# A decoder trunk on one core: five pieces of memory attention written as one stage

## The chip, the cores and the metric

The kernel runs on one core of a Trainium2 chip. A core has TensorE (PE, matrix products), VectorE (DVE), ScalarE (ACT), GpSimd (POOL) and SyncE (SP, which here only issues DMAs). The metric is the device time of one execution, in microseconds (us). Lower is better.

## The reference

One step of a one-layer trunk for 1024 prompt tokens and 8 sample tokens, model width 1024: a half-step feed-forward network, an input projection `u @ w_in`, three branches on its result (RWKV-7 time mixing, latent attention, memory cross-attention), a gated merge of the branches, and a second half-step network. The change touches the memory branch alone:

```python
def mem_kv(mem, W):                       # mem: 256 rows of 1024
    m = rmsnorm(mem, W['mem_norm'])
    k = (m @ W['mem_w_k']).reshape(B, M, MEM_HEADS, MEM_HEAD_DIM)   # 4 heads of 128; an output too
    v = (m @ W['mem_w_v']).reshape(B, M, MEM_HEADS, MEM_HEAD_DIM)   # an output too
    return k, v

def mem_attend(q, mem_k, mem_v):
    s = jnp.einsum('bqhd,bkhd->bhqk', q, mem_k).astype(jnp.float32) * (MEM_HEAD_DIM ** -0.5)
    prob = jax.nn.softmax(s, axis=-1).astype(mem_v.dtype)
    return jnp.einsum('bhqk,bkhd->bqhd', prob, mem_v).reshape(B, T, MEM_DIM)
```

The prompt's 1024 queries attend to the `k` and `v` computed here. Each of the 8 sample tokens has one query and its own cached keys and values (256 rows of 4 heads of 128, so 512 KB of keys and 512 KB of values each). All inputs and outputs are float32.

## The kernel before

The program is a row of stages (`@stage`). Each has one block with an instruction stream per engine, tied by semaphores, and ends in a barrier of all engines; inside a stage every engine runs its own list in the order written. `Steps` counts an engine's finished pieces of work, and a wait names a piece. The large arrays A, B, C, W live in one area of on-chip memory and are reused stage by stage. `k.ps[0]` to `k.ps[7]` are the eight PSUM banks, each 128 x 512 float32.

Before the change: `decode_attention` (L2143) runs the samples' attention over paged cache rows; SP issues its page loads in `pages` (L2218), and PE waits for them. Then comes the memory branch: keys, values, norm, prompt attention and sample attention, in four stages:

- `memory_keys` (L2485) loads two row tiles and both weights, turns the rows on PE (16 transposes, L2510), and ends its first block. `rms_norm` (L154, a stage of its own) squares, sums on PE, takes the root and scales. The second block makes the key and value rows with 32 float32 products of 512 columns (L2532), copies them on ACT (L2547), turns the keys (L2538) and stores both.
- `mem_attention` (L2004) loops over four heads, two in a loop body. A head's queries (516 KB) are loaded by SP, and eight tiles of 128 queries follow: score product (L2076, float32, 256 columns), maximum on DVE (L2135, L2136), exponential with its sum on ACT (L2104), reciprocal and scaling on DVE (L2138, L2139), two transposes on PE (L2083), copy on ACT (L2109), two output products (L2091), copy on ACT (L2113). POOL first starts the loads of `u_high`, `u_low` and `inv` (8.8 MB) that the next stage needs.
- `decode_memory` (L2564) does the samples: SP loads keys and values, PE spreads a query over the partitions (L2607), DVE multiplies and sums per head (L2642, L2644), a maximum over everything is taken through a PE transpose (L2610, L2612), ACT takes the exponential (L2629), PE sums (L2614), and 64 products of one column with the values as stationary operand give the result (L2620, scaled at L2662).

`tail` (L3077) follows: the merge loads its first weights (SP, L2705) and starts its products on PE.

A float32 product is two MATMUL records in the trace; a product of operands written as fp32r is one. One float32 operand is kept as a high fp32r part and a low remainder elsewhere in the kernel, and three fp32r products (high by high, high by low, low by high) stand for one float32 product.

Of the kernel before, what the change touches and what calls it, by code (L numbers as in the profile page):

```python
# [14 lines left out]
P = 128  # L15
# [1987 lines left out]
@stage  # L2003
def mem_attention(k):  # L2004


    nc = k.nc
    nq = NQ
    S2 = range(2)
    scale = MEM_SCALE  # L2010
    q_buf = [k.C[:, 13 + s, :] for s in S2]
    k_buf = [k.C[:, 15, s * MEM:(s + 1) * MEM] for s in S2]
    v_buf = [k.C[:, 16, s * 256:(s + 1) * 256].rearrange("p (t c) -> p t c", t=MTOK) for s in S2]
    prob = [k.C[:, 17 + s, 0:MEM] for s in S2]
    probT = [k.C[:, 19 + s, 0:MEM] for s in S2]

    landed = [Count(k, f"mem_q_landed{s}") for s in S2]
    order = []
    for i in range(nq + 2):
        order += [("S", i)] * (i < nq) + [("T", i - 1)] * (1 <= i <= nq) + [("O", i - 2)] * (i >= 2)  # L2020
    pe_s = Steps(k, "mem_products", [(s, x) for s in S2 for x in order], primed=True)
    act_s = Steps(k, "mem_functions", [(s, ("exp", i) if m == "S" else (m, i)) for s in S2 for m, i in order], primed=True)
    dve_s = Steps(k, "mem_softmax", [(s, x) for s in S2 for x in ["q"] + [(m, i) for i in range(nq) for m in ("max", "prob")]],
                  primed=True)
    pool_s = Steps(k, "mem_operands", [("kv", s) for s in S2])
    u_landed = Count(k, "mem_u_landed")
    chain = Count(k, "mem_chain")
    links = [0]
    per_chain = 4 * nq

    with nc.Block() as block:
        @block.sync
        def _(sp):
            with sp.Fori(0, MH // 2) as it:
                for s in S2:
                    pe_s.wait(sp, (s, ("S", nq - 1)), it, before=1)
                    sp.sem_inc(k.settled.sem, 1)
                    dve_s.wait(sp, (s, "q"), it, before=1)
                    sp.sem_inc(k.settled.sem, 1)
                    sp.dma_start(q_buf[s].rearrange("p (a t) -> p a t", a=1), k.mem_q[:, bass.ds(it * 2 + s, 1), :])\  # L2040
                        .then_inc(landed[s].sem, 16)

        @block.gpsimd
        def _(pool):
            pool.dma_start(k.XR[:, 0], k.u_high).then_inc(u_landed.sem, 16)
            pool.dma_start(k.XR[:, 1], k.u_low).then_inc(u_landed.sem, 16)
            pool.dma_start(k.inv, k.inv_spill).then_inc(u_landed.sem, 16)
            with pool.Fori(0, MH // 2) as it:
                for s in S2:
                    pe_s.wait(pool, (s, ("O", nq - 1)), it, before=1)  # L2050
                    pool.sem_inc(k.settled.sem, 1)
                    nc.gpsimd.tensor_copy(k_buf[s].rearrange("p (a t) -> p a t", a=1), k.memT[:, bass.ds(it * 2 + s, 1), :])
                    pool_s.done(nc.gpsimd.tensor_copy(v_buf[s], k.memV[:, :, bass.ds((it * 2 + s) * P, P)]), ("kv", s))
            pool.wait_ge(u_landed.sem, 48)

        @block.tensor
        def _(pe):
            def settled():

                pe.sem_inc(k.settled.sem, 1)  # L2060

            pe_s.prime(pe)
            with pe.Fori(0, MH // 2) as it:
                for s in S2:
                    if s == 0:
                        act_s.wait(pe, (1, ("O", nq - 1)), it, before=1)
                    else:
                        act_s.wait(pe, (0, ("O", nq - 1)), it)
                    pool_s.wait(pe, ("kv", s), it)
                    for m, i in order:  # L2070
                        if m == "S":
                            if i == 0:
                                dve_s.wait(pe, (s, "q"), it)
                            if i >= 2:
                                act_s.wait(pe, (s, ("exp", i - 2)), it)
                            ins = nc.tensor.matmul(k.ps[2 * (i % 2)][:, 0:MEM], q_buf[s][:, i * P:(i + 1) * P], k_buf[s],  # L2076
                                                   start=True, stop=True)
                        elif m == "T":
                            dve_s.wait(pe, (s, ("prob", i)), it)
                            if i >= 1:  # L2080
                                act_s.wait(pe, (s, ("T", i - 1)), it)
                            for b in range(MTOK):
                                ins = nc.tensor.transpose(k.ps[4][:, b * P:(b + 1) * P], prob[i % 2][:, b * P:(b + 1) * P],  # L2083
                                                          k.ident[:, :])
                        else:
                            act_s.wait(pe, (s, ("T", i)), it)
                            if i >= 2:
                                act_s.wait(pe, (s, ("O", i - 2)), it)
# [472 lines left out]


@stage
def decode_memory(k):  # L2564


    nc = k.nc
# [1567 lines left out]
```

## Time and profile before

| | us |
|---|---|
| median of 3 runs | 3678.37 (3677.28 to 3681.39) |
| the profiled execution: its time | 3683.9 |
| its span, first to last instruction | 3682.3 |
| PE busy | 3318.0 (90%) |
| DVE busy | 1646.6 (45%) |
| ACT busy | 934.9 (25%) |
| mean granted TensorE clock | 0.936 of full |

The span is the profiled execution's own; the runs without a profile are a few us shorter. Busy times are per engine and overlap. PE at 90% is a mean over stages: in the two feed-forward networks it never rests, and between them there are stretches where it waits. The granted clock is 1.00 at TensorE's full 2.4 GHz and 0.50 at 1.2 GHz; a value between is a mean over a stretch that had both.

### The profile page before, as it was taken

How to read it: one execution, taken by the hardware profiler on the slowest of the kernel's cores; microseconds unless marked ns; L12 is line 12 of the kernel's file. 1: busy time of each engine (PE TensorE's matmuls, PEld its weight loads, DVE VectorE, ACT ScalarE, POOL GpSimd, SP SyncE). 2: the span in 40 equal slices, each digit the busy share in tenths (PEclk: the TensorE clock that was granted, in tenths of full speed). 3: DMA queues.
4: the chain of work that ended last, by engine and by line, in shares of the span. 5: the costliest groups of instructions: out<-in, count | busy, mean ns of one | idle time of the engine just before them, and what ended most of it. 6: DMA issues, size and time to landing. Idle time of an engine off the chain costs nothing. (4 is left out here: it accounts for less than half of the span.)

```text
span 3682.3 us, 64108 instructions
## 1 busy us (share of the span) xinstructions
PE 3318.0 (90%) x25648; PEld 3061.6 (83%) x25648; DVE 1646.6 (45%) x2870; ACT 934.9 (25%) x1718; POOL 298.8 (8%) x402
## 2 busy tenths in 40 slices
PE   7999999989999777757897777999999899999997
PEld 7999999978998777726776545888889899999997
DVE  4445445555455333355543323222232644554555
ACT  5122122132122111214554321111123412212212
POOL 0000000031011222200001200000002300000003
PEclk8999999989999899967998886999999899999998
DMA  5111111024221100001003532211112311111102
GB/s 175 43 49 46 46 46 46 23 74 143 86 70 53 52 3 3 15 19 49 15 2 91 167 153 100 57 43 43 43 57 63 111 46 46 46 46 48 43 23 92
DMA packets 255409, 218.47 MB, mean 59 GB/s; under 512 B 39378, under 2 KB 232699, under 8 KB 254588
## 3 DMA queue, kind: packets, MB, share of 16 engines
q1 hardware_dynamic: 250684, 197.39, 17.2%
q0 software_dynamic: 3504, 18.42, 1.5%
q8 instruction: 143, 2.34, 0.3%
q14 instruction: 38, 0.31, 0.0%
q10 hardware_dynamic: 1040, 0.00, 0.0%
HBM read 179.81 MB, written 35.96 MB: 59 GB/s over the span
## 5 line engine op out<-in xcount | busy, mean ns | idle before, releaser
L1222 PE MATMUL banks<-XR,wR 128*128 128x344 f32 x6336 | 1004.2, 320 | 12.7 <-DVE XR L1455 7.9
L1222 PEld LDWEIGHTS banks<-XR,wR 128*128 128x128 f32 x6336 | 1000.0, 189 | 13.5 <-issue 10.0
L1222 PE MATMUL banks<-hidR,wR 128*128 128x344 f32 x3168 | 515.7, 323 | 6.0 <-DVE A L1354 6.0
L1222 PEld LDWEIGHTS banks<-hidR,wR 128*128 128x128 f32 x3168 | 505.4, 190 | 11.2 <-DVE A L1354 11.2
L850 PE MATMUL banks<-XR,gateR 128*128 128x344 f32 x2304 | 399.7, 331 | 14.4 <-DVE gateR L2852 7.6
L850 PEld LDWEIGHTS banks<-XR,gateR 128*128 128x128 f32 x2304 | 372.8, 191 | 29.5 <-DVE gateR L2830 7.9
L1354 DVE TENSOR_TENSOR A<-A,banks 128x344 f32<-128x344 f32 x528 | 264.4, 511 | 192.5 <-PE banks L1222 191.5
L850 PE MATMUL banks<-XR,pR 128*128 128x344 f32 (+1 forms) x1944 | 317.6, 325 | 8.0 <-DVE XR L1455 4.4
L850 PEld LDWEIGHTS banks<-XR,pR 128*128 128x128 f32 (+1 forms) x1944 | 311.6, 191 | 15.0 <-issue 10.8
L1307 ACT ACTIVATE sq<-sq 128x344 f32<-128x344 f32 x132 | 65.1, 493 | 1005.3 <-DVE sq L1334 1005.3
L1334 DVE TENSOR_TENSOR sq<-banks,shared 128x344 f32<-128x344 f32 x132 | 68.2, 516 | 417.9 <-PE banks L1222 417.9
L979 POOL TENSOR_TENSOR rs<-rs,sq 128x344 f32<-128x344 f32 x63 | 59.3, 942 | 2096.4 <-ACT sq L968 2092.4
L1326 DVE TENSOR_TENSOR wR<-wraw,wR 128x2048 fp32r<-128x2048 f32 (+1 forms) x66 | 147.0, 2228 | 54.9 <-ACT wR L1303 54.9
L402 PE MATMUL banks<-C 64*64 64x64 f32 x3840 | 139.3, 224 | 27.6 <-DVE C L552 11.3
L402 PEld LDWEIGHTS banks<-C 64*64 64x64 f32 x3840 | 127.9, 139 | 38.3 <-issue 38.3
L2838 DVE TENSOR_TENSOR sq<-banks,shared 128x344 f32<-128x344 f32 x72 | 37.2, 517 | 261.3 <-PE banks L2743 261.3
L2781 ACT ACTIVATE sq<-sq 128x344 f32<-128x344 f32 x72 | 35.4, 491 | 369.1 <-DVE sq L2838 369.1
L402 PE MATMUL banks<-W 64*64 64x64 f32 (+1 forms) x1280 | 97.5, 278 | 32.7 <-issue 17.6
L1303 ACT ACTIVATE wR<-wraw 128x2048 fp32r<-128x2048 f32 (+1 forms) x66 | 122.3, 1854 | 0.2
L402 PEld LDWEIGHTS banks<-W 64*64 64x64 f32 x1280 | 91.6, 161 | 33.7 <-issue 33.7
L2743 PE MATMUL banks<-A,w_o 128*128 128x344 f32 x384 | 118.8, 452 | 0.0
L1311 ACT ACTIVATE hidR<-rs 128x344 fp32r<-128x344 f32 x132 | 64.9, 492 | 151.4 <-DVE rs L1341 151.4
(410 smaller groups left out, 3778.6 us busy)
## 6 DMA issues: line engine op xcount, KB each, us to landing
wraw<-in_ffn_down SPq DMA_DIRECT2D x22, 1024.0 KB, 4.9
wraw<-in_ffn_gate SPq DMA_DIRECT2D x43, 512.0 KB, 3.7
wraw<-in_ffn_up SPq DMA_DIRECT2D x43, 512.0 KB, 4.8
praw<-in_w_in SPq DMA_DIRECT2D x26, 512.0 KB, 4.3
C<-in_cache_mla SPq DMA_DIRECT2D x64, 144.0 KB, 2.7
C<-in_cache_mla POOLq DMA_DIRECT2D x64, 144.0 KB, 2.9
B<-h_spill SPq DMA_DIRECT2D x6, 1376.0 KB, 10.1
h_spill<-A SPq DMA_DIRECT2D x6, 1376.0 KB, 6.3
```

The source lines that it names most:

```text
L402: return nc.tensor.matmul(out, lhsT, rhs, start=start, stop=stop)
L850: ins = k.nc.tensor.matmul(out, parts[:, a, cols], k.XR[:, b, f, grp(g)], start=first and n == 0, stop=last and n == 2)
L979: self.pool_s.done(self.k.nc.gpsimd.tensor_tensor(self.acc[g], self.acc[g], self.slot[g, f], ALU.add), (g, f))
L1222: ins = self.k.nc.tensor.matmul(out, wgt[:, a, cols], x(b)[:, grp(g)], start=first and n == 0, stop=last and n == 2)
L1303: self.act_s.done(nc.scalar.activation(self.wr[u][:, 0, 0:n], self.raw[u][:, 0:n], ACT.Copy), m)
L1307: self.act_s.done(nc.scalar.activation(self.sig[g], self.z[g], ACT.Sigmoid), ("sig", t, g))
L1311: self.act_s.done(nc.scalar.activation(k.hidR[:, 0, t, grp(g)], self.h[g], ACT.Copy), ("hi", t, g))
L1326: self.dve_s.done(nc.vector.tensor_tensor(self.wr[u][:, 1, 0:n], self.raw[u][:, 0:n], self.wr[u][:, 0, 0:n].bitcast(F32), ALU.subtract), m)
L1334: self.dve_s.done(nc.vector.tensor_tensor(self.z[g], k.ps[2 * (n % 2)][:, 0:TG], k.inv[:, grp(g)], ALU.mult), ("z", t, g))
L1354: self.dve_s.done(nc.vector.tensor_tensor(k.A[:, j, grp(g)], k.A[:, j, grp(g)], k.ps[4 + n % 4][:, 0:TG], ALU.add), ("dn", g, j))
L2743: ins = k.nc.tensor.matmul(k.ps[2 * at + 1][:, 0:TG], self.w_o[b][:, f], self.branches[b][0][:, f, grp(g)], start=(f == 0), stop=(f == 3))
L2838: steps.done(nc.vector.tensor_tensor(k.t3[:, at, :], k.ps[2 * at][:, 0:TG], k.inv[:, grp(g)], ALU.mult), ("gate",) + m)
```

## The change

`memory_keys`, its `rms_norm`, `mem_attention` and `decode_memory` are gone, and one stage `memory` does their work, without barriers inside and without loops.

- Loads ahead: at the end of `decode_attention`, SP also issues the memory rows and the key weights (3 MB, into B). The value weights, the queries of all heads (2 MB, one transfer), and the samples' cache rows follow in the new stage; the cache rows go through a ring of seven 512 KB slots, where eight had been loaded for values and four reused for keys.
- Norm: ACT takes the squares' row sums straight from the rows (no PE sums); the gain is applied by DVE as it copies the turned rows, and the inverse root by the copies of key rows (DVE) and value rows (ACT).
- Samples beside the products: a query is spread between the key and value products; DVE multiplies and sums meanwhile.
- Scores: queries and keys are split into high and low fp32r parts, with the scale and a minus sign in the query, so a minimum is the bias as it is; three fp32r products replace one float32 product.
- Two query tiles a step, sixteen steps: scores two steps ahead, exponentials one ahead; one reduction, two exponentials, one reciprocal, two scalings, four transposes, one copy of 512 columns, two output products of 256 columns, one copy.
- Waits of a step n: PE's transposes wait for DVE's scaled n, its scores n + 2 for ACT's exponential n, its output products for ACT's copy of the transposes n and for the output copy n - 1. ACT runs exponential n + 1, copy n, output copy n; DVE runs minimum n + 2, scaling n + 1. The samples' pieces lie inside steps: a maximum through PE in steps 0 and 1, the sum in step 2, output products before `output` in steps 4 and 6, their copies on ACT in steps 5 and 7, and the turning back (PE, DVE) in steps 8 and 9.
- Sample output: weights padded to 32 columns are the stationary operand and the values the moving one; four samples use four groups of 32 output partitions, 16 products of 512 columns in all, then eight transposes.
- `u_high` is loaded after the value products, `u_low` after the last sample product (it shares room with three of the ring slots).

The removed functions are printed above. The core of what is added:

```diff
@@ decode_attention, SP
             for n in range(2, N):
                 pages(sp, n, 0)
+            for dst, src in k.mem_loads:
+                sp.dma_start(dst, src).then_inc(k.mem_ahead.sem, 16)
@@ memory, SP
+            def fetch(i):
+                if i >= RING:
+                    if i - RING < DEC:
+                        dve_s.wait(sp, ("s", i - RING))
+                    else:
+                        pe_s.wait(sp, "o%d" % ((i - RING) % DEC // 4))
+                sp.dma_start(slots[i % RING], cache_rows(i)).then_inc(ring_landed[i % RING].sem, 16)
+            sp.dma_start(k.qm_dec[:, :, :], k.mem_q[:, :, SEQ:T]).then_inc(landed_q.sem, 16)
+            for i in range(2):
+                fetch(i)
+            sp.dma_start(w_v, k.io["mem_w_v"][0].rearrange("(f p) n -> p f n", p=P)).then_inc(landed_v.sem, 16)
+            for i in range(2, 4):
+                fetch(i)
+            sp.dma_start(k.mem_raw, k.mem_q[:, :, 0:SEQ]).then_inc(landed_all_q.sem, 16)
+            for i in range(4, 2 * DEC):
+                fetch(i)
@@ memory, POOL
+            pe_s.wait(pool, ("V", 1))
+            pool.dma_start(k.XR[:, 0], k.u_high).then_inc(u_landed.sem, 16)
...
+            pe_s.wait(pool, "o1")
+            pool.dma_start(k.XR[:, 1], k.u_low).then_inc(u_landed.sem, 16)
@@ memory, PE, setup
+            rows("K", w_k, 0, 5)
+            laid(0)
+            laid(1)
+            rows("K", w_k, 1, 6)
+            laid(2)
+            laid(3)
+            keys_turned(0)
+            pe.wait_ge(landed_v.sem, 16)
+            rows("V", w_v, 0, 2)
+            laid(4)
+            laid(5)
+            keys_turned(1)
+            rows("V", w_v, 1, 3)
+            laid(6)
+            laid(7)
@@ memory, PE, a step
+            def score(n):
...
+                for x in X2:
+                    at = (2 * j + x) * P
+                    for m, (a, b) in enumerate(((0, 0), (0, 1), (1, 0))):
+                        ins = nc.tensor.matmul(k.ps[n % 2][:, x * MEM:(x + 1) * MEM], k.mem_qp[a][:, h, at:at + P],
+                                               k.mem_kT[:, b, h, :], start=(m == 0), stop=(m == 2))
...
+            def sample_out(z):
...
+                        ins = nc.tensor.matmul(k.ps[6 + z][32 * s:32 * s + 32, :], scz[:, b, t, :],
+                                               slots[(DEC + b) % RING][:, t, :], start=(t == 0), stop=(t == MTOK - 1))
...
+            score(0)
+            score(1)
+            for n in range(STEPS):
+                turn(n)
+                if n + 2 < STEPS:
+                    score(n + 2)
...
+                output(n)
@@ memory, ACT, a step
+            exponent(0)
+            for n in range(STEPS):
+                if n + 1 < STEPS:
+                    exponent(n + 1)
+                pe_s.wait(act, ("t", n))
...
+                act_s.done(nc.scalar.activation(k.mem_pT[:, n % 2, :], k.ps[2 + n % 2], ACT.Copy), ("t", n))
...
+                pe_s.wait(act, ("o", n))
...
+                act_s.done(nc.scalar.activation(out[:, h, 2 * j * P:(2 * j + 2) * P], k.ps[5][:, 0:2 * P], ACT.Copy), ("o", n))
@@ memory, DVE, setup and steps
+            sampled(0)
+            sampled(1)
+            keys(0)
+            sampled(2)
+            keys(1)
+            sampled(3)
+            keys_low(0)
+            sampled(4)
+            sampled(5)
+            query_low(0)
+            query_low(1)
+            sampled(6)
+            keys_low(1)
+            sampled(7)
+            query_low(2)
+            query_low(3)
...
+            top(0)
+            top(1)
+            scaled(0)
+            for n in range(STEPS):
+                if n + 2 < STEPS:
+                    top(n + 2)
+                if n + 1 < STEPS:
+                    scaled(n + 1)
@@ build
-        memory_keys(k, v["mem_norm"])
-        mem_attention(k)
-        decode_memory(k)
+        memory(k, v["mem_norm"])
         tail(k, v)
```

## Rows read from the trace of the kernel before

**Rows 1.** The page, part 1: engine, busy us, share of the span, instructions.

```profile
PE 3318.0 (90%) x25648; PEld 3061.6 (83%) x25648; DVE 1646.6 (45%) x2870; ACT 934.9 (25%) x1718; POOL 298.8 (8%) x402
```

**Rows 2.** Windows by stage: from:to, length, busy us (instructions) per engine, granted clock, DMA.

```profile
2106.00:2127.00 21.00, 8.04 (x37) 7.12 (x37) 5.25 (x14) 6.63 (x14) 0.00 (x0) 0.58 0.70 250
2127.00:2160.00 33.00, 31.01 (x72) 13.85 (x72) 0.00 (x0) 3.37 (x6) 0.00 (x0) 0.92 0.09 33
2160.00:2168.00 8.00, 0.05 (x1) 0.05 (x1) 0.17 (x1) 1.28 (x1) 3.01 (x7) 0.67 0.75 271
2168.00:2239.00 71.00, 49.94 (x256) 35.06 (x256) 33.37 (x131) 35.03 (x129) 1.49 (x4) 0.89 0.31 126
2239.00:2269.00 30.00, 18.27 (x26) 5.48 (x27) 20.45 (x20) 0.84 (x2) 0.00 (x0) 0.54 0.75 280
2269.00:2297.00 28.00, 27.25 (x129) 27.16 (x128) 0.79 (x3) 0.00 (x0) 0.00 (x0) 0.50 0.00 1
2297.00:2304.00 7.00, 0.14 (x1) 0.14 (x1) 1.23 (x1) 1.10 (x2) 0.00 (x0) 0.50 0.87 231
```

**Rows 3.** Timeline, first instruction of the memory stages: start us, length, engine, line.

```profile
2106.26 0.83 SPq L2501 DMA_DIRECT2D W<-in_mem_prompt  x2
```

**Rows 4.** Timeline, the last of the memory stages and the first after.

```profile
2296.35 0.21 DVE L2662 TENSOR_TENSOR C<-banks,W 128x32 f32<-128x32 f32 x1 [26.66 <-PE banks L2620]
...
2297.33 0.38 SPq L2705 DMA_DIRECT2D C<-in_w_in  x1
```

**Rows 5.** Timeline, prompt attention, two tiles in a row.

```profile
2229.67 0.42 DVE L2135 TENSOR_REDUCE nmax<-banks 128x1 f32<-128x256 f32 x1
...
2231.38 0.42 DVE L2135 TENSOR_REDUCE nmax<-banks 128x1 f32<-128x256 f32 x1
```

**Rows 6.** Groups by line and shape, 2091 to 2304 us: xcount, busy us, mean ns.

```profile
L2532 PE MATMUL banks<-C 128*128 128x512 f32 x64 | 30.2, 635 | 4.3 <-PEq L53 4.3
...
L2091 PE MATMUL banks<-C 128*128 128x128 f32 x128 | 21.7, 295 | 0.8 <-ACT C L2109 0.8
...
L2607 PE MATMUL banks<-W,ident 8*128 8x512 f32 x16 | 16.0, 1114 | 4.5 <-DVE W L2644 3.8 <-ACT W L2627 0.7
...
L2104 ACT ACTIVATE C<-banks,nmax 128x256 f32<-128x256 f32 x32 | 15.1, 473 | 34.7 <-DVE nmax L2136 34.7
...
L2083 PE MATMUL banks<-ident,C 128*128 128x128 f32 x64 | 15.1, 320 | 17.4 <-DVE C L2139 16.6 <-DVE qm_dec L2131 0.8
...
L2135 DVE TENSOR_REDUCE nmax<-banks 128x1 f32<-128x256 f32 x32 | 13.4, 420 | 9.8 <-PE banks L2076 9.8
...
L2109 ACT ACTIVATE C<-banks 128x256 f32<-128x256 f32 x32 | 12.0, 374 | 3.0 <-PE banks L2083 3.0
...
L2139 DVE TENSOR_SCALAR C<-C,rsum 128x256 f32<-128x256 f32 x32 | 11.3, 353 | 1.1
...
L2642 DVE TENSOR_TENSOR C<-spare_w,banks 128x1024 f32<-128x1024 f32 x8 | 9.8, 1222 | 9.4 <-DMA spare_w<-in_cache_mem_k 9.0
...
L2644 DVE TENSOR_REDUCE W<-C 128x8 f32<-128x1024 f32 x8 | 9.8, 1220 | 0.3
...
L2547 ACT ACTIVATE C<-banks 128x512 f32<-128x512 f32 x4 | 2.4, 598 | 34.2 <-PE banks L2532 34.2
```

**Rows 7.** Timeline, PE: 48 fp32r products of 256 columns (prompt latent attention).

```profile
1886.56 5.92 PE L3594 MATMUL banks<-mla_w,XR 128*128 128x256 f32 x48
```

**Rows 8.** Timeline, PE: eight float32 products, 32 output partitions each (page attention).

```profile
2039.32 1.05 PE L2315 MATMUL banks<-C,sq 128*32 128x256 f32 x16
```

**Rows 9.** Window of 4 us in prompt attention, its first head.

```profile
2172.00:2176.00 4.00, 3.76 (x15) 2.83 (x14) 2.19 (x8) 1.59 (x8) 0.00 (x0) 0.50 1.10 462
```

**Rows 10.** Timeline, SP: the last loads of cache pages.

```profile
2061.92 25.65 SPq L2218 DMA_DIRECT2D C<-in_cache_mla  x18
```

**Rows 11.** DMA issues, 2091 to 2304 us: xcount, KB each, median us to landing.

```profile
XR<-u_low POOLq DMA_DIRECT2D x1, 4128.0 KB, 25.0
...
C<-in_mem_w_v SPq DMA_DIRECT2D x1, 2048.0 KB, 15.2
```

More of the change, by code:

```diff
@@ L2143, in decode_attention @@
-@stage
 def decode_attention(k):
@@ L3257, in _ @@
             fin.copy_low(dve, 2)
+STEPS = MH * NQ // 2
 def shape_constants():
@@ L4059, in build @@
         k.mla_wk_raw = at("mla_wk_raw", [P, KT * P], at_k + 4 * SEQ + 2 * P)
+        at_m = 2 * DT * T + 12 * T
+        k.mem_kT = at("mem_kT", [P, 2, MH, MEM], at_m, R32)
+        k.mem_v = at("mem_v", [P, MTOK, 512], at_m + 2048)
+        k.mem_raw = at("mem_raw", [P, MH, SEQ], at_m + 3072)[:, :, :]
+        k.mem_qp = [at("mem_q_high", [P, MH, SEQ], (2 * DT + FT) * T, R32), at("mem_q_low", [P, MH, SEQ], at_m + 3072, R32)]
+        k.mem_prob = at("mem_prob", [P, 2, 2, MEM], at_m + 7168)
+        k.mem_pT = at("mem_pT", [P, 2, 512], at_m + 8192)
+        k.mem_so = at("mem_so", [P, 2, 512], at_m + 9216)
         k.mla_v = at("mla_v", [P, NQ, 2 * P], DT * T)
@@ L4066, in build @@
         k.settled = Count(k, "products_may_start")
+        k.mem_ahead = Count(k, "memory_rows_and_weights_ahead")
+        flat_b = k.B[:, :, :].rearrange("p a t -> p (a t)")
+        k.mem_loads = [(flat_b[:, t * D:(t + 1) * D], k.io["mem_prompt"][0, t * P:(t + 1) * P, :]) for t in range(MTOK)]
+        k.mem_loads += [(flat_b[:, 2 * D:2 * D + 4096].rearrange("p (f c) -> p f c", f=DT),
+                         k.io["mem_w_k"][0].rearrange("(f p) n -> p f n", p=P))]
         k.u_high = nc.dram_tensor("u_high", [P, DT, T], F32).ap()
@@ L4072, in build @@
         k.s_dec = k.q_dec[:, 0:RT, :]
-        k.memT = k.C[:, 12, 0:MH * MEM].rearrange("p (h t) -> p h t", h=MH)
-        k.memV = k.C[:, 21, 0:MTOK * 512].rearrange("p (t c) -> p t c", t=MTOK)
+        k.memV = k.mem_v[:, :, :]
+        k.mem_scz = k.spare_w[:, 7168:7680].rearrange("p (b t h) -> p b t h", b=DEC, t=MTOK)
         k.Bc = k.C[:, 2:22, :].rearrange("p a t -> p (a t)")[:, 0:4 * (NPAGE + 1) * CW]\
```

574 lines of the change are left out of this document (282 added, 292 removed).

## The prediction, made before the changed kernel ran

> **What bounds the kernel now.** I read the page's busy times first, then the windows, then the timeline, then the groups. PE is busy 3318.0 of 3682.3 us [rows 1], so only a stretch in which PE rests, runs at the half clock or does avoidable work can be worth much. The windows by stage show such a stretch [rows 2]. The memory stages begin at 2106.26 [rows 3] and the first load of the next stage is issued at 2297.33 [rows 4]: 191.1 us. In them the reader is to see four kinds of loss:
> - 2106 to 2127: PE is busy 8.04 of 21 us; loads, norm and barriers.
> - 2160 to 2168: PE is busy 0.05 of 8 us; the queries are loading.
> - 2168 to 2239: no engine is full (PE 49.9, DVE 33.4, ACT 35.0 of 71 us). Two tiles start 1.71 us apart [rows 5], and that is a round between two engines: maximum 0.42, exponential 0.47, scaling 0.35 [rows 6], and 0.47 for the small instructions and semaphores between them. DVE does not start the next maximum before the scaling.
> - 2239 to 2297: the clock is 0.54 and then 0.50, first under DVE's sample work (20.45 of 30 us), then under 128 MATMULs of one column, which hold PE for 27.25 us. The last DVE instruction waited 26.66 us for them [rows 4].
> Nothing of another stage overlaps this stretch, so what it loses in length the kernel loses.
>
> **The setup of the new stage.** Times are counted from its first instruction (2106.3 before).
> Products: the 32 float32 products of 512 columns took 30.2 us [rows 6]; the clock of 0.92 over 33 us [rows 2] is 5.3 us at half speed, so 2.6 us are clock and one product is (30.2 - 2.6) / 32 = 0.86 us at full clock. A record's mean of 0.635 against a spacing of 0.43 gives 0.2 us of drain after a group. These products stay. A transpose is 15.1 / 64 = 0.24 us; a spread of a query took 16.0 / 8 = 2.0 us, at the half clock [rows 2, 6], and as a float32 product of 512 columns I take 0.86 at full clock. DVE needs 2 x 1.22 and a gap, 2.6 us, per sample.
> PE's order, end by end: 20 transposes 4.8; key product 0 with the same 2.6 us of half clock 14.3; two spreads 16.0; key product 1 22.9; two spreads 24.6; turning 25.1; value product 0 32.0; two spreads 33.7; turning 34.2; value product 1 41.1; two spreads 42.8. DVE follows: samples 0 to 5 fit under PE (the last pair spread by 33.7, done 39, then two query lows of 1.2 us each by 41.4); sample 6 at 44.6, key low 45.3, sample 7 47.9, two query lows 50.4, the samples' maximum and the first minimum 51.3, exponentials 0 at 52.4, scaling 0 at 53.3. So the first turn of the loop starts at 53.3. The bounds: 41 us, PE's work alone, if DVE kept up; 60 if spreads stay near 2.0 and the half clock lasts longer. I take 53.3, since every term but the clock has its row. ACT's squares, root, copies and query highs (12 pieces of 0.6 to 1.1 us) lie inside the products; without that cover they would cost about 10.
>
> **The loop.** A step is two tiles. Two circles can close it.
> PE to DVE: four transposes 0.5; six fp32r products, 48 of which took 5.92 us [rows 7], so 6 x 0.123 = 0.74, and 0.2 drain; minimum over 512 elements 0.69 (between 0.42 for 256 and 1.22 for 1024); reciprocal and two scalings 0.9; semaphore 0.1. Sum 3.1.
> ACT to PE: two exponentials 0.94, copy of 512 columns 0.60, semaphore 0.2, two output products of 0.43 each (half of 0.86) with drain 1.06, copy 0.37. Sum 3.2.
> PE's own work is 0.5 + 0.74 + 0.86 = 2.1 us and hidden in either. From below the step is 2.6 (the circles opened by work that runs ahead), from above 2 x 1.71 = 3.4, no better than now. I take 3.1. Fifteen steps from the first turn to the last: 46.5. After the last turn: 0.6 + 0.6 + 1.06 + 0.4 = 2.8 with semaphores. The minus sign and the scale in the query save one small DVE instruction a tile; that is in the step.
> Extras in the loop, mostly on one of the circles: maximum through PE 0.5 and 1.0 (steps 0, 1), sum, reciprocals and weights 1.2 (step 2), sample products 2 x 1.9, their copies 2 x 0.6, turning back 2 x 0.7. Sum 9.1. The sample product rests on a row: eight float32 products of 256 columns with 32 output partitions each took 1.05 us [rows 8], where eight of 0.43 in a row would be 3.4; so four groups run together, and eight of 512 columns are 2 x 0.86 + 0.2 = 1.9. Were they not together it would be 6.9 each, 10 us more. They replace the 27.4 us of the old output.
>
> **Clock at the loop's start.** Before the first turn PE rests from about 47 (score 1) to 53.3. After the rest at 2160 PE worked at 0.50 in a 4 us window although it was busy 3.76 of it [rows 9], and the mean to 2239 is 0.89 [rows 2]. I add three steps at the half clock, where PE's terms double and a step is 4.3: 3.4 us. The ends are 0 and all steps (rival 2).
> The Trainium skill (TensorE: Matmul & The Clock Gate, Part 4) says that transposes do not count as activity for the clock. By that rule the loop would be likelier to stay at the low level; it gives rival 2 its place. The old attention loop, with two transposes for every three float32 products, has 0.89 in its row.
>
> **Transfers.** The rows and key weights go behind the last page load, which is issued at 2061.92 + 25.65 = 2087.6 [rows 10]. In the old stage 2 MB landed 15.2 us after issue with 3 MB ahead of them [rows 11]; 3 MB issued at 2087.6 are there by 2102.8, before 2106.3. Nothing of the page loop is queued behind them, since they are issued last; the last page shares the wires with them, 0 to 0.5 us. Without this cover the stage would start some 5 us later. The value weights and the queries are 6.1 MB with what is ahead of them; at the 462 GB/s of [rows 9] that is 13 us, at the 271 GB/s of the load-in 23, and they are wanted at 25.1 and 33. Ring slots are refilled by samples done long before: key 7 waits for sample 0, values for samples 1 to 7, and only the last value waits for the first sample product, two steps before its use. On POOL, `u_high` starts at 41. `u_low` waits for the second sample product, 53.3 + 7 x 3.1 + 7 = 82, and with the 25.0 us of [rows 11] is there at 107, before the end. This is the thinnest cover, 8 us; each us beyond it lengthens the stage.
>
> **Sum.** 53.3 + 46.5 + 2.8 + 9.1 + 3.4 + 0.8 (stage end to the next issue, as 2296.56 to 2297.33 in [rows 4]) = 115.9 us against 191.1: 75 us less. The next stage begins with a load and a half clock as before, so nothing more. The profiled execution took 3683.9, so 3609 by its own time; the median of the runs is 5.5 lower, so 3603.
>
> **Rivals.**
> 2. The loop stays at 1.2 GHz: 15 x 1.2 more, 4 on the extras, less the 3.4 counted: 18.6 less gain, 3622. If the setup does so too (27.5 - 2.6 for the products, 9 for the spreads): 34 more, 3656. For it: after 2269 PE is busy 27.25 of 28 us at 0.50, so a busy PE is not always granted 1.00. Against it: key and value products stood at a mean of 0.92, the old loop at 0.89 with a like mix [rows 2].
> 3. The samples are not hidden: each spread waits for the DVE piece two before it, and if products and DVE take turns, 8 x 2.6 = 20.8 return, and with steps of 3.4 another 4.8: gain 49.6, 3629. For it: strict order on every engine. Against it: the order above leaves each spread ready when its turn comes.
> 4. Slower than before: the code of the loop is now straight and must itself be brought in by DMA, in the first 25 us behind 6 MB of data and from 41 on behind `u_high`. If an engine stands at a block of instructions that lands like `u_low`, 25.0 us after its request [rows 11], three such stops eat the 75 us; five would give 3603 + 125 = 3728. Against it: the page attention is straight code too, and its PE products in [rows 8] ran without a gap.
> The Trainium skill (Runtime: NRT & Kernel Launch, Instruction fetch mechanics) says that sequential fetch runs ahead and is mostly hidden, and that a taken branch is what breaks it; by it this rival is nothing.
> 5. The change doesn't do what it says, and another circle (output copy waits for `output`, which waits for the sample product) makes the steps as long as now: within 7 us of zero it could only come out if the setup grew by 60 too.
>
> **How the numbers follow.** Forecast 0.66; rival 2 in the loop 0.16, whole 0.04; rival 3 0.10; rival 4 0.03; rival 5 0.01. The time is the forecast's, 3603. Its own low end is steps of 2.6 and a shorter setup: 7.5 + 5 + 3 less, 3587; the range takes 3585 to 3632, so that rival 2 in the loop and rival 3 are in it. A measurement of this kernel tells 0.2% (7.4 us) from no change. Faster by more: 0.66 + 0.16 + 0.04 + 0.10 less a little, 0.95; same 0.02; slower 0.03.
>
> **What would show it.** The stretch from the first product's transposes to the merge's first load is 116 us; the first scaled tiles come 53 us into it; minima of two-tile steps are 3.1 us apart; key and value products take 30 us in all; a sample product takes 1.9 us; the clock is 1.00 after the first three steps; no wait of PE for a load, and none of the last barrier for `u_low`. The prediction is wrong if steps take 4 us, if PE waits for `laid` or the ring, or if the stretch after 2300 changes its length.

## The result, and the profile after

| | before | after |
|---|---|---|
| median of 4 runs, us | 3679.88 (3677.28 to 3685.25) | 3592.55 (3588.57 to 3601.47) |
| ratio, 95% interval | | 0.9757 (0.9742 to 0.9773) |
| profiled execution: span | 3682.3 | 3594.7 |
| first load of the memory stages to the merge's first load | 191.1 | 103.6 |

The kernel is 2.4% faster: 87.3 us by the medians, 87.6 by the spans. The forecast was 3603 (75 us less), the range 3585 to 3632. The whole difference lies in the stretch: 191.07 - 103.58 = 87.5 us. What follows it has the same length within 1.1 us (1385.0 from the merge's first load to the end of the span before, 1383.9 after).

PE's line of the page, part 1, answers to [rows 1]; PE lost 55 us of busy time, the largest part of it, 24 us, with the one-column products (27.4 us before, two sample products of 1.86 after), and 8 with the spreads (16.0 before, 7.9 after):

```profile
PE 3263.0 (91%) x25508; PEld 3022.9 (84%) x25508; DVE 1639.7 (46%) x2809; ACT 930.2 (26%) x1681; POOL 298.8 (8%) x399
```

The setup, in the timeline of the kernel after (start us, length, engine, line). L3771 are the transposes of the memory rows, L4020 the minimum, L3838 the transposes of a step, called a turn here:

```profile
2091.07 0.43 SPq L2103 DMA_DIRECT2D B<-in_mem_w_k  x1
...
2107.21 0.63 SPq L3736 DMA_DIRECT2D qm_dec<-mem_q  x1
...
2107.26 3.65 PE L3771 MATMUL banks<-ident,B 128*128 128x128 f32 x16 [1.23 <-PEq L53]
```

```profile
2155.69 1.28 DVE L4020 TENSOR_REDUCE rms_col<-banks 128x2 f32<-128x512 f32 x2
...
2158.34 1.12 PE L3838 MATMUL banks<-ident,mem_prob 128*128 128x128 f32 x4 [4.26 <-DVE mem_prob L4028]
```

```profile
2209.63 0.38 ACT L3951 ACTIVATE C<-banks 128x256 f32<-128x256 f32 x1 [1.22 <-PE banks L3847]
2210.79 0.38 SPq L2390 DMA_DIRECT2D C<-in_w_in  x1
```

The key weights are on their way from 2091, and PE starts 0.05 us after the first load of the stage. The first turn of the loop comes at 2158.34, 51.1 us into the stage (forecast 53.3), and the last one at 2207.17 is followed by the merge's load 3.6 us later, as forecast (2.8 + 0.8). Between them are 48.8 us where 59.0 had been forecast.

The windows by part of the new stage (from:to, length; busy us and instructions of PE, its weight loads, DVE, ACT and POOL; granted clock, DMA share, GB/s), to set beside [rows 2]:

```profile
2107.00:2128.00 21.00, 20.74 (x56) 10.71 (x56) 8.38 (x10) 4.36 (x7) 1.07 (x2) 0.87 0.92 334
2128.00:2152.00 24.00, 21.54 (x57) 9.55 (x57) 17.20 (x16) 7.52 (x9) 2.69 (x5) 0.96 0.72 255
2152.00:2158.00 6.00, 2.07 (x10) 1.78 (x9) 5.44 (x10) 1.59 (x7) 0.00 (x0) 0.50 0.96 372
2158.00:2162.00 4.00, 3.66 (x14) 3.37 (x15) 1.48 (x6) 0.94 (x3) 0.00 (x0) 0.50 0.92 313
2162.00:2166.00 4.00, 3.89 (x19) 3.00 (x18) 2.10 (x8) 1.95 (x7) 0.00 (x0) 0.78 0.82 326
2166.00:2170.00 4.00, 3.46 (x25) 3.11 (x26) 2.09 (x7) 2.56 (x11) 0.00 (x0) 1.00 0.00 0
2170.00:2209.00 39.00, 31.20 (x202) 23.79 (x201) 16.50 (x55) 22.57 (x74) 0.54 (x1) 1.00 0.31 123
2209.00:2217.00 8.00, 0.59 (x3) 0.19 (x1) 1.23 (x1) 1.44 (x2) 0.00 (x0) 0.66 0.67 181
```

PE is busy 42.3 of the first 45 us. Then it is busy 2.07 of the 6 us from 2152 to 2158 while DVE, busy 5.44 of them, ends the samples and the low parts; the granted clock is 0.50 (1.2 GHz) there and until 2162, 0.78 to 2166, and 1.00 (2.4 GHz) from then to 2209, the end of the loop; in the window after it, with PE busy 0.59 of 8 us, it is 0.66.

A step in its steady state, from the same timeline:

```profile
2195.15 0.60 PE L3838 MATMUL banks<-ident,mem_prob 128*128 128x128 f32 x4
2195.35 0.39 ACT L3951 ACTIVATE C<-banks 128x256 f32<-128x256 f32 x1 [1.22 <-PE banks L3847]
...
2195.51 0.48 PE L3826 MATMUL banks<-mem_kT,mem_q_high 128*128 128x256 f32 x2
2195.64 0.47 ACT L3930 ACTIVATE mem_prob<-banks,rms_col 128x256 f32<-128x256 f32 x1
...
2196.50 0.69 DVE L4020 TENSOR_REDUCE rms_col<-banks 128x2 f32<-128x512 f32 x1 [1.59 <-PE banks L3826]
2196.53 0.60 ACT L3941 ACTIVATE mem_pT<-banks 128x512 f32<-128x512 f32 x1
...
2197.19 1.13 PE L3847 MATMUL banks<-mem_pT,mem_v 128*128 128x256 f32 x4 [0.73 <-ACT mem_pT L3941]
2197.30 0.61 DVE L4028 TENSOR_SCALAR mem_prob<-mem_prob,rms_col 128x256 f32<-128x256 f32 x2
...
2198.16 0.60 PE L3838 MATMUL banks<-ident,mem_prob 128*128 128x128 f32 x4
2198.36 0.38 ACT L3951 ACTIVATE C<-banks 128x256 f32<-128x256 f32 x1 [1.22 <-PE banks L3847]
...
2198.64 0.47 ACT L3930 ACTIVATE mem_prob<-banks,rms_col 128x256 f32<-128x256 f32 x1
```

ACT starts an exponential at 2195.64, a copy at 2196.53, PE its output products at 2197.19, ACT their copy at 2198.36 and the next exponential at 2198.64: 3.00 us round. ACT rests 1.22 us of it, waiting for PE (in brackets in the answer's row), PE rests 0.73 waiting for ACT, and DVE rests 1.59 before its minimum. DVE's minimum follows the scores and its scaling ends at 2197.91, 0.25 before the next turn.

Groups of the stage (xcount, busy us, mean ns, idle before), the answers to [rows 6]:

```profile
L3847 PE MATMUL banks<-mem_pT,mem_v 128*128 128x256 f32 x64 | 18.8, 419 | 7.8 <-ACT mem_pT L3941 7.8
...
L3790 PE MATMUL banks<-rs,ident 8*128 8x512 f32 x16 | 7.9, 613 | 0.0
...
L3782 PE MATMUL banks<-B 128*128 128x512 f32 x32 | 14.7, 613 | 0.0
```

A spread took 7.9 / 8 = 0.99 us, the output products waited 7.8 us for ACT's copies, and the key and value products took 14.7 + 14.1 = 28.8 us.

The first sample product in PE's timeline:

```profile
2173.24 0.62 PE L3858 MATMUL banks<-C,spare_w 128*32 128x512 f32 x2
2173.26 0.62 PE L3858 MATMUL banks<-sq,spare_w 128*32 128x512 f32 x2
...
2174.56 0.60 PE L3858 MATMUL banks<-C,spare_w 128*32 128x512 f32 x2
2174.57 0.60 PE L3858 MATMUL banks<-sq,spare_w 128*32 128x512 f32 x2
2175.10 1.13 PE L3847 MATMUL banks<-mem_pT,mem_v 128*128 128x256 f32 x4
```

It runs from 2173.24 to the next product's start at 2175.10, 1.86 us (forecast 1.9): eight products of 512 columns in four groups side by side.

### The profile page after: what moved, and what is told of

Read it like the earlier page. It is cut to its first block and busy times, and to the rows that moved or that the text cites. A ratio compares the mean times of both kernels' runs of the same rounds, so it can differ in the third digit from the quotient of the medians.

```text
span 3594.7 us, 63286 instructions
## 1 busy us (share of the span) xinstructions
PE 3263.0 (91%) x25508; PEld 3022.9 (84%) x25508; DVE 1639.7 (46%) x2809; ACT 930.2 (26%) x1681; POOL 298.8 (8%) x399
## 5 line engine op out<-in xcount | busy, mean ns | idle before, releaser
L850 PE MATMUL banks<-XR,gateR 128*128 128x344 f32 x2304 | 398.2, 330 | 14.7 <-DVE gateR L2537 7.9
L402 PEld LDWEIGHTS banks<-C 64*64 64x64 f32 x3840 | 130.3, 141 | 36.6 <-issue 36.6
```

The lines of the kernel that those rows point to most:

```text
L402: return nc.tensor.matmul(out, lhsT, rhs, start=start, stop=stop)
L850: ins = k.nc.tensor.matmul(out, parts[:, a, cols], k.XR[:, b, f, grp(g)], start=first and n == 0, stop=last and n == 2)
```

## The experiments

All start from the changed kernel. For each, the table gives the stretch (the stage's first load to the merge's first load), the time from the stage's first load to the first turn, from the first turn to the last, and the usual step, all from its profile. The effects of most are a few us, under what a single run's time can tell: the start of the stage alone lay between 2100.09 and 2112.24 from run to run, mostly by the page loads before it (the last of them is issued between 2081.5 and 2094.2). The stretch is free of that. Two profiles of the changed kernel gave 103.58 and 103.37.

| kernel | stretch | to first turn | first to last turn | step |
|---|---|---|---|---|
| the changed kernel | 103.6 | 51.1 | 48.8 | 3.00 |
| e1, no sample pieces | 100.9 | 51.3 | 46.0 | 2.87 to 3.01 |
| e2, loads in the stage | 117.5 | 64.9 | 49.0 | 3.00 |
| e3, samples after | 111.8 | 59.9 | 48.3 | 3.00 |
| e4, old output | 122.0 | 51.2 | 67.2 | 3.00 |
| e5, float32 scores | 100.6 | 47.7 | 49.3 | 3.03 |
| e6, late copy | 101.3 | 51.0 | 46.7 | 2.87 |
| e7, minimum after scaling | 103.7 | 51.2 | 48.9 | 3.00 |
| e8, output a step later | 91.8 | 50.8 | 36.6 | 2.01 |
| e9, setup order | 100.7 | 48.4 | 48.7 | 3.00 |
| e10, e8 and e9 | 91.1 | 49.1 | 37.7 | 2.01 |
| e11, one tile an instruction | 104.2 | 50.3 | 50.2 | 3.12 |

My theory, once the profile was there: the parts of the change are right, and the term of the extras is not. What is laid into a loop that one circle closes costs only what exceeds the rest of its engine. The rival was the way of counting in the prediction, and for the loop, another circle than ACT's.

**e1, are the extras free?**

```diff
-    extra = {0: ["mT"], 1: ["mB"], 2: ["sum"], 4: ["o0"], 6: ["o1"], 8: ["turn0"], 9: ["turn1"]}
+    extra = {}
```

(and the same on ACT and DVE)

> The changed kernel without the samples' pieces inside the loop of sixteen steps (maximum through PE, difference, exponential, sum, weights, the sixteen output products, their copies and the turning back); the samples' part of the output is left out, the setup is as it was. Theory (slack): a step is closed by ACT to PE to ACT (two exponentials, copy of 512 columns, two output products, output copy; 3.0 us), and PE and DVE rest in it, so that pieces laid there cost only what exceeds the rest. Then the time from the first turn to the last falls from 48.8 to about 46.7 us and the stretch from the stage's first load to the merge's first load from 103.6 to about 101.5. Rival (the term of the prediction): each piece adds its own length, 9.1 us together; then the stretch falls to about 94.5.

The stretch fell by 2.7 us to 100.9, the time between the turns by 2.8. So all sample pieces in the loop cost 2.8 us, not 9.1. (The samples' output is missing here, so this is no kernel to use.) In the changed kernel a step with a sample product takes 4.06 instead of 3.00, so 1.86 us of products cost 1.06; the steps with copies on ACT (5 and 7) and with the turning back (8 and 9) take 3.00 like the others. Without the pieces the steps 2 to 6 take only 2.87 to 2.92: PE's turn waits for DVE's scaling there (0.43 us, then less from step to step), until PE waits for ACT's copy instead (0.73 at the end) and the step is 3.00. Two circles of nearly the same length lie side by side.

**e2, the loads ahead.**

```diff
@@ decode_attention, then memory, SP
-            for dst, src in k.mem_loads:
-                sp.dma_start(dst, src).then_inc(k.mem_ahead.sem, 16)
...
+            for dst, src in k.mem_loads:
+                sp.dma_start(dst, src).then_inc(k.mem_ahead.sem, 16)
             sp.dma_start(k.qm_dec[:, :, :], k.mem_q[:, :, SEQ:T]).then_inc(landed_q.sem, 16)
```

> The changed kernel with the loads of the memory rows and key weights (3 MB) issued at the start of the new stage instead of behind the last cache pages. Theory: PE and ACT wait for all three transfers; 2 MB behind 1 MB landed 11.9 us after issue in the changed kernel, so the first transposes come about 9 to 10 us later and nothing of that is won back: stretch 103.6 to about 113, page attention unchanged. The prediction's number was some 5 us: 109. Rival: the other loads are pushed back too and the setup waits for the queries, so that it is more than 12 us.

Timeline of this kernel:

```profile
2111.62 1.29 SPq L3735 DMA_DIRECT2D B<-in_mem_prompt  x2
...
2125.12 2.18 PE L3771 MATMUL banks<-ident,B 128*128 128x128 f32 x9 [14.69 <-DMA B<-in_mem_w_k]
```

PE starts 13.5 us after the first load, and the stretch is 13.9 longer; the rest of the setup has its old length (51.4 us from PE's start to the first turn, 51.1 before). Neither number was right. The key weights are issued 1.3 us after the stage's first load and took 12.1 us to land, and PE waits for all of it; with the stage's other loads issued right behind them they were hardly slower than the 11.9 us of the changed kernel. This part of the change is worth 13.9 us, nearly three times what the prediction said for its cover. It costs the page attention nothing that shows: from the issue of the last page load to the stage's first load it is 17.4 us in this kernel, 18.7 in the kernel before, and 17.2 to 19.2 in those with the 3 MB issued ahead.

**e3, samples beside the products.**

```diff
-            sampled(0)
-            sampled(1)
             keys(0)
-            sampled(2)
             keys(1)
...
+            for b in B8:
+                sampled(b)
```

(the same order in `laid` on PE; the low parts come before the samples)

> The changed kernel with the samples' spreads and their DVE work all after the four products of keys and values, the rest in the old order. Theory: the products come 6 spreads (5.7 us) earlier, then DVE needs 8 x 2.57 = 20.6 us, while keys' and queries' low parts are already done: the first minimum comes about 6 us later than in the changed kernel, and PE, resting longer, starts the loop at the half clock for longer, 1 to 3 us: stretch 103.6 to 111 to 113. Rival (price of the prediction's rival 3): laying the samples beside the products hides their whole 20.8 us: stretch about 124.

8.2 us longer, as the theory had it: 8.7 of it up to the first turn, 0.5 won back behind it. The clock at the loop's start was no worse (48.3 from turn to turn). Laying the samples beside the products is worth 8 us and not 21, because the spreads push the products back (the value products end 39.5 us into the stage in the changed kernel, 33.4 here) and DVE's last pieces are bare in either order (7.0 us from PE's last spread to the first minimum in the changed kernel).

**e4, the old output form.**

```diff
-                        ins = nc.tensor.matmul(k.ps[6 + z][32 * s:32 * s + 32, :], scz[:, b, t, :],
-                                               slots[(DEC + b) % RING][:, t, :], start=(t == 0), stop=(t == MTOK - 1))
+                            ins = nc.tensor.matmul(k.ps[6 + z][:, s * MH + h:s * MH + h + 1],
+                                                   slots[(DEC + b) % RING][:, t, h * P:(h + 1) * P], scz[:, b, t, h:h + 1],
+                                                   start=(t == 0), stop=(t == MTOK - 1))
```

> The changed kernel with the samples' output in the old form: 128 MATMUL records of one column with the values as stationary operand, in steps 4 and 6, in place of the sixteen products in four column groups; no turning back. The old form took 27.4 us at the half clock, 0.43 us a product. Theory: its cost is the weight loading and goes with the clock, so here at full clock 0.21 a product, 13.7 us for all 64, less the 2.1 that the new products cost: stretch 103.6 to about 115. Rival: one-column products let the clock fall to 0.50 and stay 0.43: 27 us, stretch about 129.

PE's timeline, and the windows around it, of this kernel:

```profile
2174.67 3.63 PE L3858 MATMUL banks<-spare_w,C 128*128 128x1 f32 x32
2178.16 6.23 PE L3858 MATMUL banks<-spare_w,sq 128*128 128x1 f32 x32
2184.25 2.05 PE L3847 MATMUL banks<-mem_pT,mem_v 128*128 128x256 f32 x4
```

```profile
2171.00:2176.00 5.00, 4.28 (x35) 3.92 (x33) 2.50 (x9) 3.29 (x12) 0.00 (x0) 1.00 0.02 3
2176.00:2184.00 8.00, 8.00 (x52) 8.00 (x52) 0.29 (x2) 0.00 (x0) 0.00 (x0) 0.69 0.00 0
...
2196.00:2200.00 4.00, 4.00 (x22) 4.00 (x21) 0.00 (x0) 0.00 (x0) 0.00 (x0) 0.51 0.01 4
```

18.4 us longer, between the two. The first 32 records take 3.63 us (0.11 each, half of the old 0.21 a record), the next 32 take 6.23. In the window from 2176 PE is busy 8.00 of 8 us at a granted 0.69, and from 2196 at 0.51. So both theories are true one after the other: a record costs by the clock, with the weight loads busy as long as PE (8.00 of 8 us too), and in this loop, whose clock stays at 1.00 without the form, the clock falls under it while PE never rests.

**e5, float32 scores.**

```diff
-                    for m, (a, b) in enumerate(((0, 0), (0, 1), (1, 0))):
-                        ins = nc.tensor.matmul(k.ps[n % 2][:, x * MEM:(x + 1) * MEM], k.mem_qp[a][:, h, at:at + P],
-                                               k.mem_kT[:, b, h, :], start=(m == 0), stop=(m == 2))
+                    ins = nc.tensor.matmul(k.ps[n % 2][:, x * MEM:(x + 1) * MEM], k.mem_qp[0][:, h, at:at + P].bitcast(F32),
+                                           k.mem_kT[:, 0, h, :].bitcast(F32), start=True, stop=True)
```

(and no `keys_low`, `query_low`)

> The changed kernel with one float32 product for a tile's scores in place of three fp32r products, and without the low parts of queries and keys on DVE. Theory: in the loop PE rests 0.73 us a step before the output products, and four records of 256 columns at a quarter rate are 0.85 us against 0.65 to 0.75 now, so the step stays 3.0; in the setup DVE has two query lows (2.4) and a key low (0.7) less between the last spread and the first minimum: stretch 103.6 to about 100.5. Rival: the circle PE score, DVE minimum, DVE scaling, PE turn is as tight as ACT's, and the longer score makes the step 3.1 to 3.2: the gain of the setup is given back.

100.6 against 100.5 expected. The first turn is 3.5 us earlier and the loop 0.5 longer. The split in three fp32r products loses 3 us here: PE has the time for the float32 ones in the loop, and DVE, which makes the low parts, is the engine that ends the setup.

**e6 and e7, which circle closes the step?**

```diff
@@ e6: ACT
-                pe_s.wait(act, ("o", n))
+                    pe_s.wait(act, ("o", n - 1))
@@ e6: PE
-                if n:
-                    act_s.wait(pe, ("o", n - 1))
+                if n >= 2:
+                    act_s.wait(pe, ("o", n - 2))
...
-                    ins = nc.tensor.matmul(k.ps[5][:, 0:2 * P], k.memV[:, t, n // 4 * P:(n // 4 + 1) * P],
+                    ins = nc.tensor.matmul(k.ps[(5, 7)[n % 2]][:, 0:2 * P], k.memV[:, t, n // 4 * P:(n // 4 + 1) * P],
@@ e7: DVE
-                    top(n + 2)
                 if n + 1 < STEPS:
                     scaled(n + 1)
+                if n + 2 < STEPS:
+                    top(n + 2)
```

> The changed kernel with ACT's output copy one step later, behind the next exponentials and the next copy of transposes, and the output products in two banks in turn. This opens the circle through ACT. Theory: the circle turn n, score n+2, minimum n+2, scaling n+1, turn n+1 stands at 2.9 in the trace (2195.15 to 2198.04) and closes the step then: 2.9 us, stretch about 102. Rival: ACT's circle was the only one, and the step falls to what PE or ACT need, 2.2: stretch about 92.

> The changed kernel with DVE's minimum of a step behind the scaling of the step before, as in the old loop, so that DVE and ACT take turns again; still two tiles a step. Theory: that round is two exponentials 0.99, reciprocal and scalings 0.81, minimum 0.69 and semaphores, about 2.6 us, less than the 3.0 that ACT's circle takes: nothing changes in the loop (48.8 from first to last turn), and running ahead was worth nothing, two tiles an instruction was the gain. Rival: running ahead broke the old round, and without it two tiles take 2 x 1.71 = 3.4 again: 6 us more.

Both came out by the theory. With ACT's circle open the step is 2.87: the circle of turn, score, minimum, scaling was right behind it, and PE's turn now waits for DVE, as it did not before. A turn in PE's timeline of e6:

```profile
2174.83 0.66 PE L3839 MATMUL banks<-ident,mem_prob 128*128 128x128 f32 x4 [0.40 <-DVE mem_prob L4034]
```

With DVE's run-ahead taken back nothing changes (103.7, 48.9). So the run-ahead of the minimum, which looks like the heart of the new loop, is worth nothing in this order of PE and ACT.

**e11, is it the width of the instructions?**

```diff
-                act_s.done(nc.scalar.activation(k.mem_pT[:, n % 2, :], k.ps[2 + n % 2], ACT.Copy), ("t", n))
+                for x in X2:
+                    ins = nc.scalar.activation(k.mem_pT[:, n % 2, x * 2 * P:(x + 1) * 2 * P],
+                                               k.ps[2 + n % 2][:, x * 2 * P:(x + 1) * 2 * P], ACT.Copy)
+                act_s.done(ins, ("t", n))
```

(the same for the minimum and the output copy)

> The changed kernel with the same order and the same work, but the minimum, the copy of the transposes and the output copy each as two instructions of one tile in place of one of two tiles. Theory: the circle through ACT holds two of them; two copies of 256 columns are 2 x 0.37 against 0.60 and two of 128 are 2 x 0.28 against 0.38, with some overlap of neighbours 0.25 more in all: the step goes from 3.0 to 3.2 or 3.3, first to last turn from 48.8 to 52 to 54. So wider instructions are worth some 4 us and the rest of the loop's gain is that two tiles share a round. Rival: the width is the gain, and two tiles take 3.4 or more again: 55 or more.

A step takes 3.12: even less than the theory's 3.2. Two instructions of half the width in three places cost 0.12 us a step more. So most of the loop's gain, 3.12 us with narrow instructions against 2 x 1.71 [rows 5], lies in what this kernel keeps: two tiles that share a round with its waits, scores and exponentials issued further ahead, and one small DVE instruction a tile less. No run tells the shares of these apart.

**e8, both circles open.**

```diff
@@ PE
-            for n in range(STEPS):
-                turn(n)
+            for n in range(STEPS + 1):
                 if n + 2 < STEPS:
                     score(n + 2)
+                if n < STEPS:
+                    turn(n)
...
-                output(n)
+                if n:
+                    output(n - 1)
```

(ACT's output copy as in e6, one bank)

> The changed kernel with PE's order in a step as scores n+2, transposes n, output products n-1, and ACT's output copy a step later too. This opens both circles: no engine waits in its step for what another makes in the same step. Theory: the step falls to 2.2 to 2.4 (PE 1.95 of products and transposes), from first to last turn 48.8 to about 38, stretch about 93. Rival: another circle (exponential n, score n+2, minimum, exponential n+2) or the single bank of the output holds the step at 2.8 or more: stretch 100 or more.

Timeline of this kernel, ACT and PE:

```profile
2191.59 0.47 ACT L3934 ACTIVATE mem_prob<-banks,rms_col 128x256 f32<-128x256 f32 x1
...
2191.82 0.60 PE L3840 MATMUL banks<-ident,mem_prob 128*128 128x128 f32 x4
...
2192.26 1.03 PE L3849 MATMUL banks<-mem_pT,mem_v 128*128 128x256 f32 x4
...
2192.49 0.60 ACT L3946 ACTIVATE mem_pT<-banks 128x512 f32<-128x512 f32 x1
...
2192.93 0.59 PE L3828 MATMUL banks<-mem_kT,mem_q_high 128*128 128x256 f32 x2
...
2193.32 0.38 ACT L3957 ACTIVATE C<-banks 128x256 f32<-128x256 f32 x1 [0.23 <-PE banks L3849]
...
2193.60 0.47 ACT L3934 ACTIVATE mem_prob<-banks,rms_col 128x256 f32<-128x256 f32 x1
...
2193.84 0.60 PE L3840 MATMUL banks<-ident,mem_prob 128*128 128x128 f32 x4
```

From turn to turn 2.01 us, below the theory's 2.2, and PE goes from transposes to output products to scores without a wait. The stretch is 91.8: 11.8 us less than the changed kernel. In the old loop the output products already came a step behind the transposes (its order on PE was scores i, transposes i - 1, output products i - 2); the change had moved them into the same step, and with that laid its own circle.

This kernel also shows the other half of e1, since PE does not rest in its steps. PE's timeline, the turns before and after the second sample product:

```profile
2176.86 0.60 PE L3840 MATMUL banks<-ident,mem_prob 128*128 128x128 f32 x4
...
2180.91 0.60 PE L3840 MATMUL banks<-ident,mem_prob 128*128 128x128 f32 x4
```

That step takes 4.05 us against 2.01, so a sample product costs its whole length, 2.04, where it cost 1.06 in the changed kernel; and a step with a turning back takes 2.44, 0.43 more, where it cost nothing.

**e9 and e10, the setup, and a version that beats both.**

```diff
             query_low(0)
-            query_low(1)
-            sampled(6)
             keys_low(1)
+            query_low(1)
+            sampled(6)
             sampled(7)
-            query_low(2)
-            query_low(3)
...
+                if n in (3, 4):
+                    query_low(n - 1)
```

> The changed kernel with DVE's setup in another order alone: the key low before the second query low and the last two samples, the query lows of heads 2 and 3 in steps 3 and 4. Theory: the first turn comes 2.4 to 2.6 us earlier, since DVE ends the setup and two query lows of 1.2 leave it, and in the loop DVE rests 1.6 us a step before its minimum, so they cost nothing there: stretch 103.6 to about 101.1. Rival (the prediction's way of counting extras): they cost their 2.4 us in the loop, and nothing is won: 103.5.

> The changed kernel once more, for its ratio to the kernel before on the chip on which the next one runs too. Both theories: 0.976 of before, a stretch of 103.6 us.

> The changed kernel with the output a step later on PE and ACT (which alone gave a stretch of 91.8) and the setup in another order on DVE (the key low before the second query low and the last two samples, the query lows of heads 2 and 3 in steps 3 and 4). Theory: the first minimum comes 2.4 us earlier; in steps of 2.0 DVE is busy 1.5 and a query low of 1.2 does not fit, so that about 1.4 of it come back: stretch about 91, and the kernel 12 to 13 us, 0.35%, faster than the changed kernel: 0.9725 of before. Rival: the earlier start finds the clock at 1.2 GHz for as long as before, and what is left of it is lost in the first steps: stretch 92 to 93.

e9 is 2.9 us shorter, 2.7 of it before the first turn; in the loop the two query lows cost nothing (48.7). In e10, where steps are 2.0 us, they cost 1.1 (37.7 against 36.6), and only 1.7 is won before the first turn. Over five rounds on one chip the changed kernel ran at 0.9757 (0.9741 to 0.9772) of before, 3597.33 us, and e10 at 0.9709 (0.9696 to 0.9722), 3578.77 us. So e10 beats both, by 0.5% the changed one; the stretch explains 12.2 of the 18.6 us between the medians. The rest lies within the intervals, and e10's profile has its memory stage starting 8.3 us earlier, which the page loads do from run to run; it is not shown to be a gain.

## Why the prediction was right, and where it was off

**What bounds it.** Right. The stretch held the gain, nothing else moved, and the four losses named were there to be had. Taken back one by one, the loads ahead (13.9), the samples beside the products (8.2) and the new output form (18.4) make 40.5 of the 87.5 us. No run takes back the loop of two tiles as a whole, the barriers, the norm or the load of all queries at once, so the other 47 are not divided among them.

**Setup, 53.3 forecast, 51.1 measured.** The order held: PE ends the value products and spreads, DVE ends the setup. The key and value products took 28.8 us, near 27.5 + 2.6. A spread took 0.99 and not 0.86. The first minimum waited for the samples and query lows, as said, and e3, e5 and e9 each moved it by the DVE work that they moved.

**The step, 3.1 forecast, 3.00 measured.** Right in size, and right that two circles lie close together: the circle through ACT closes it (forecast 3.2, measured 3.00), with the one through DVE 0.13 behind (forecast 3.1, measured 2.87 in e6). But since both must close, the prediction should have taken the longer of its two, 3.2, and it took 3.1. It also named as a loss of the old loop that DVE does not start the next maximum before the scaling; e7 shows that this order, put back, costs nothing here.

**The extras, 9.1 forecast, 2.8 measured (e1).** This is the term that failed, and 6.3 of the 12.3 us by which the stretch was shorter than forecast. The prediction wrote "Extras in the loop, mostly on one of the circles" and summed their lengths. They are in fact on engines that rest in each step (PE 0.73, ACT 1.22, DVE 1.59 us), and a piece costs only its excess; where PE does not rest (e8), a piece on it does cost its length, as the prediction counted.

**The clock, 3.4 forecast.** The first two steps took 4.10 and 3.47, together 1.6 us over 3.00 (1.5 in e1, without pieces in them); the windows have 0.50 up to 2162 and 0.78 up to 2166, so less than two steps at the half clock and not three. So this term was 1.8 too large. (Three steps of 4.3 instead of 3.1 would be 3.6, not the 3.4 written.) With 15 x 0.1 of the step's term, 2.2 of the setup and the 6.3 of the extras that makes 11.8 of the 12.3. The 0.5 left comes from setting the pieces' price by e1: five of its steps lie below 3.00, 0.6 us in all, and against steps of 3.00 the pieces cost 2.2, not 2.8. The Trainium skill (TensorE: Matmul & The Clock Gate, Part 4) says that the full clock doesn't engage for transposes, since they don't count as busy in the same way. Here 64 transposes lie among the products, and the granted clock was 1.00 over the 39 us from 2170; so rival 2, for which the prediction took the rule to speak, did not come about. No run here shows transposes alone.

**The transfers.** The thinnest cover, `u_low`, held: the merge's first load was issued 0.8 us after the last copy's end, the forecast's stage end without a wait. The cover was about twice the 8 us forecast: `u_low` was issued at 2182.8, the DMA engines moved 438 GB/s from 2190 to 2194 and nothing from 2194 to 2196, so it was there at most 11 us after its issue (an estimate from these windows; 25 had been taken), 16 before the end. For the loads ahead the prediction said that without them the stage would start "some 5 us later"; e2 measured 13.9. The 5 was the wait of the old stage, whose first load came at 2106.26 [rows 3] and which needed only the first 1 MB for its transposes:

```profile
2111.10 3.67 PE L2510 MATMUL banks<-ident,W 128*128 128x128 f32 x16 [6.03 <-DMA W<-in_mem_prompt]
```

The new stage waits for all 3 MB.

**The rivals.** 2 and 4 did not occur: the clock rose, and all longer waits of PE, ACT and DVE in the stage end with another engine's work (but for PE's 1.23 us at the stage's start, and 2.0 us of DVE that the profile puts down to nothing and that end when PE's spread of the seventh sample is done). 3 was overpriced: the samples after the products cost 8 us more (e3), not 20.8, since the spreads between the products cost 6 and DVE's last 7 us were bare anyway. 5 fell with the measured stretch.

## What to carry to other kernels

Find the circle that closes a step before pricing what is put into it: work on an engine that rests in each step costs its excess over the rest (1.06 of 1.86 us), and work on an engine that never rests costs its whole length (2.04, e8). When a loop has several engines in turn, let each use what the others made a step earlier; that took the step from 3.00 to 2.01 us here, more than wider instructions (0.12) or the run-ahead of one engine alone (0). And split an operand only where the split's maker is not the engine that ends the stage.

## What the runs showed of the hardware

- Under matrix products of one column with a 128 x 128 stationary operand PE was busy all the time (8.00 of 8 us), and still the granted clock came down from 1.00 to 0.69 and then 0.51 (e4). A record took 0.11 us at 1.00 and 0.21 at 0.50 (kernel before); in e4 32 records took 3.63 us and the next 32, with the fall among them, 6.23.
- Eight float32 products of 512 columns with 32 output partitions each took 1.86 us in four column groups.
- A 16 KB transfer landed 2.1 us after issue in the changed kernel and 11.8 us in e2, where 3 MB had been issued on the same queue just ahead.
